# Early products between the steps of the chains: whole groups of eight tiles at every second place in place of half groups at each

## What is computed

```python
for l in range(2):
    z = rmsnorm(x) @ w_in[l]          # all branches and merge gates
    o_a = gated_delta_rule(...)       # branch A: 4 heads, triangular solve in chunks
    o_b = latent_attention(...)       # branch B: 8 heads, prompt causal, samples over 2048 past tokens
    o_c = mlstm_chunked(...)          # branch C: 4 heads
    x += w_out(sum_b sigmoid(gate_b) * (o_b @ w_branch_b))
    x += down(silu(causal_dwconv3(gate) + bias) * up)
```

## Time and profile before

| | |
|---|---|
| median of 3 runs | 1474.86 us (1474.51 to 1476.02) |
| the profiled execution | 1478.7 us, its span 1476.9 us |
| PE busy | 1379.1 us (93%), 7716 matmul records |
| DVE busy | 491.4 us (33%) |
| ACT busy | 273.5 us (19%) |
| POOL busy | 178.4 us (12%) |
| mean granted TensorE clock | 0.973 |

### The profile page before, as it was taken

How to read it: one execution, slowest core, us unless ns; L and a number is a source line. 1 busy time by engine, 2 the same in 40 slices (tenths; PEclk the granted TensorE clock), 3 DMA queues, 4 the chain that set the end, 5 groups by cost and what they waited for, 6 DMA issues and landing times.

```text
span 1476.9 us, 18904 instructions
## 1 busy us (share of the span) xinstructions
PE 1379.1 (93%) x7716; PEld 1140.3 (77%) x7716; DVE 491.4 (33%) x1163; ACT 273.5 (19%) x646; POOL 178.4 (12%) x230
## 2 busy tenths in 40 slices
PE   3999989999999899989989999899999979999894
PEld 3878967777887788878768799677688868888783
DVE  2764255422121333320048434562211223333101
ACT  1331132422100111100014212243220011111000
POOL 1014234120000000000100241442000000000000
PEclk9989999999999999999989899999999999999997
DMA  6422237441343244444444223564224424444320
GB/s 247 143 91 72 86 94 260 162 185 58 121 151 133 100 148 152 142 134 142 140 152 136 69 72 93 194 214 173 99 81 147 137 97 142 152 148 144 133 100 30
DMA packets 58278, 194.82 MB, mean 132 GB/s; under 512 B 7440, under 2 KB 7504, under 8 KB 55120
## 3 DMA queue, kind: packets, MB, share of 16 engines
q1 hardware_dynamic: 49248, 149.97, 30.4%
q0 software_dynamic: 8944, 43.64, 8.5%
HBM read 184.32 MB, written 9.25 MB: 131 GB/s over the span
## 4 chain that ended last, share of the span: by engine, by line
PE 92%; DVE 3%; ACT 2%; issue 1%; DMA 1%; POOL 0%; DVEq 0%; ACTq 0%; POOLq 0%
PE banks L515 70%; PE banks L956 2%; PE banks L634 1%; PE banks L555 1%; PE banks L649 1%; PE banks L962 1%; PE banks L583 1%; PE banks L862 1%; PE banks L1006 1%; PE banks L965 1%; DVE arena L1436 1%; DMA arena<-in_x 1%; PE banks L623 1%; PE banks L950 1%; PE banks L657 1%
## 5 line engine op out<-in xcount | busy, mean ns | idle before, releaser
L515 PE MATMUL banks<-arena 128*128 128x264 f32 x4576 | 1058.4, 391 | 33.8 <-DVE arena L1436 22.8
L515 PEld LDWEIGHTS banks<-arena 128*128 128x128 f32 x4576 | 870.6, 192 | 199.5 <-DVE arena L1436 24.5
L1083 ACT ACTIVATE arena<-banks 128x512 f32<-128x512 f32 (+6 forms) x296 | 119.8, 432 | 524.4 <-PE banks L515 338.9
L1926 DVE TENSOR_SCALAR arena<-arena 128x256 f32<-128x256 f32 x44 | 18.2, 414 | 157.6 <-ACT arena L1083 157.6
L2127 POOL COPY arena<-arena 128x2 f32<-128x2 f32 x44 | 14.0, 317 | 406.3 <-ACT arena L1083 406.3
L1955 DVE SCALAR_TENSOR_TENSOR arena<-banks,arena 128x264 f32<-128x264 f32 x16 | 6.9, 433 | 155.0 <-PE banks L515 155.0
L555 PE MATMUL banks<-arena 128*128 128x264 f32 x64 | 20.6, 490 | 24.3 <-ACT arena L1119 19.3
L2028 POOL TENSOR_TENSOR arena<-arena 128x512 f32<-128x512 f32 x28 | 30.8, 1120 | 84.5 <-PE banks L634 47.3
L555 PEld LDWEIGHTS banks<-arena 128*128 128x128 f32 x64 | 15.5, 249 | 29.0 <-issue 19.7
L1114 ACT ACTIVATE arena<-banks 128x264 f32<-128x264 f32 x32 | 12.6, 392 | 129.4 <-PE banks L515 129.4
L1616 DVE TENSOR_TENSOR arena<-arena,banks 128x512 f32<-128x512 f32 x24 | 16.4, 689 | 55.2 <-PE banks L649 52.6
(11 more groups left out here) (402 smaller groups left out, 1188.5 us busy)
## 6 DMA issues: line engine op xcount, KB each, us to landing
arena<-in_weights SPq DMA_DIRECT2D x230, 512.0 KB, 3.2
arena<-in_weights SPq DMA_DIRECT2D x112, 256.0 KB, 3.1
arena<-in_s POOLq DMA_DIRECT2D x2, 2048.0 KB, 13.0
out_ss_o<-arena POOLq DMA_DIRECT2D x16, 256.0 KB, 3.2
arena<-in_mla_w POOLq DMA_DIRECT2D x4, 1024.0 KB, 8.2
arena<-in_c POOLq DMA_DIRECT2D x4, 512.0 KB, 6.0
out_sc_o<-arena POOLq DMA_DIRECT2D x16, 128.0 KB, 2.7
arena<-in_x POOLq DMA_DIRECT2D x1, 1056.0 KB, 11.2
```

The lines of the kernel that those rows point to most:

```text
L515: mm = nc.tensor.matmul(dst, ring[:, at_:at_ + 128], rhs[:, j, :], start=(start and j == 0), stop=(stop and j == k - 1))
L1083: return A(dst, src, ACT.Copy, scale=scale)
L1926: link(ts(cv, fc[:, j % 3, 0:TP], w[0], par[:, Q_FB + j:Q_FB + j + 1], ALU.mult, ALU.add))
```

## The change

A class `Owed` counts the halves that are due and those that are done. `half(n)` adds n to those due, and then does only as many as make whole groups; a half that is left over is owed until the next place. The same rule stands in `schedule()` and in the blocks of PE, ACT and DVE. Since `wa` and `wc` are single halves, where they come the count shifts by one.

```diff
+class Owed:
+    def __init__(self):
+        self.due = self.done = 0
+
+    def take(self, n):
+        self.due += n
+        at = self.done
+        while at < len(PIECES):
+            end = at + 1 + LAST_PIECE[at:].index(True)
+            if end > self.due:
+                break
+            at = end
+        n, self.done = at - self.done, at
+        return range(n)
...
-                piece, early = [0], [None]
+                piece, early, owed = [0], [None], Owed()
 
                 def half(n):
 
-                    for _ in range(n):
+                    for _ in owed.take(n):
                         k = piece[0]
                         name, i, parts, _ = PIECES[k]
...
-                half(len(PIECES) - piece[0])
+                half(len(PIECES) - owed.due)
                 b = claim("ov", 0, ("cmb", 1))
```

More of the change, by code:

```diff
@@ L89 @@
 assert sorted(STREAM) == list(range(2 * UNITS))
+class Owed:
[11 more added lines that the diff above has]
+        return range(n)
 def schedule():
-    s, piece = [], [0]
+    s, piece, owed = [], [0], Owed()
     def add(name, n=1, reader="A", first=0):
@@ L154, in schedule @@
     add("ss", 1, "A", 1); half(2); add("mxT", 1, "V", 1); half(1); add("mxB", 1, "V", 1); half(3); add("ptx", 1, "A", 1)
-    half(1); add("lsum", 1, "V", 1); add("cx", 1, "A", 1); half(3); add("cmb", 1, "V", 1); half(len(PIECES) - piece[0])
+    half(1); add("lsum", 1, "V", 1); add("cx", 1, "A", 1); half(3); add("cmb", 1, "V", 1); half(len(PIECES) - owed.due)
     add("ov")
@@ L1083, in copy @@
                     return A(dst, src, ACT.Copy, scale=scale)
-                piece = [0]
+                piece, owed = [0], Owed()
                 def half(n):
-                    for _ in range(n):
+                    for _ in owed.take(n):
                         name, i, _, reader = PIECES[piece[0]]
```

## The result

The changed kernel takes 1510.19 us (median of four runs, 1509.28 to 1511.77), the kernel before 1475.44 beside it (four runs, 1474.51 to 1476.3). The ratio is 1.0233, with a 95% interval of 1.022 to 1.0247: slower by 34.7 us. The forecast was 1500.2, with a range of 1490 to 1508; the direction is right, the size too small by 10 us.

A forecast was written before the change was run, and what follows sets the result against it. PE was taken to bound the kernel, its waits paid in full. Lost cover of 11.0 us a layer, +22 for both, plus 3.3 of clock gave 1504.0 for the profiled execution and 1500.2 for the median, range 1490 to 1508.

The forecast's parts named there:

- `l2`, +1.78: From `l2` to the broadcasts: PE's 1.89 us wait grows by the whole moved half, +1.78 us a layer.
- `T` to `TT`, 0.6 each: Levels 1, 3 and 5: `TT`'s second chunk waits for DVE's copy, 0.6 us each, +1.8 a layer.
- `ks` to `vn1`, +1.4: `vn1` is reached at 186.35 but must wait for DVE's four operations, ending at 187.68: +1.4 us a layer.
- `os` to `mn0`, +1.78: PE's 4.05 us wait for DVE ahead of `mn0` grows by the half moved behind `mc1`, +1.78 us a layer.
- `mq`, -0.3: Between `mout` and `mq` two halves stand where one was, so the 0.3 us wait goes: -0.3 a layer.
- `mxT`, +1.4: `mxT` of page 3 has one half fewer ahead and waits for DVE's maximum: +1.4 us a layer.
- the rival by the weight loads: Each of nine uncovered places outside the long waits costs 0.15 us more, 2.8 over both layers: 1503; no chance given.
- the clock: Low clock after the grown waits at `l2` and `mn0`, two in each layer: 0 to 6.6 us in all, +3.3 taken.
- against the runs: Profiled execution lay 3.8 us above the median, so 1504.0 for it was put at 1500.2 for the median.
- only the long waits count: Rival: places at `TT`, `vn0`, `vn1` and the pages are free, 4.8 us a layer: 1484.4, with some clock 1486; 8%.
- More low clock: Rival: every grown wait brings one more low stretch and `l2` two, 22 + 10 = 32 us: 1507; 12%.
- Faster: Rival: clock returns at once or low stretches fall into longer waits, 9.3 us won: 1471.6; 2%.

The follow-up runs named there:

- chain kernel: Kernel before with only the halves in the seven levels and at `vn0`, `ks`, `vn1` made whole groups; traces from `vT` to `o1` take 4.56 and 4.90 us more.
- second trace: Both kernels run again unchanged in a later sitting: the kernel before 1476.5 us (ratio 1.0002), the changed kernel 1511.76 us (ratio 1.024).
- four part kernels: Kernel before with one part each: half behind `l2` moved, half ahead of `mn0` moved, levels to `vn1` whole, or pages whole; together 40.4 us slower.

## Why the prediction fell short

Step by step, with the starts of the steps in layer 0:

1. *`l2`, +1.78*: 1.78 of cover, right, with 0.65 of low clock beside it.
2. *`Y` to `T`, +0.1 for both*: 0.06 and 0.07. Right.
3. *`T` to `TT`, 0.6 each*: 0.63, 0.63, 0.62. Right. In layer 1 the one at level 3 costs 0.34 more, in the chain kernel too: its second chunk waits 0.59 us for 0.23, with the granted clock at 1.00. No run shows why DVE is later there.
4. *`vn0`, +1.0*: 1.05. Right.
5. *`ks` to `vn1`, +1.4*: 1.48. Right; all four operations of DVE count.
6. *`os` to `mn0`, +1.78*: 1.78, right, with 0.22 of clock.
7. *`mq`, -0.3*: -0.15. The half's cover was mis-sized by 0.15.
8. *`mxT`, +1.4*: 1.56 of cover, and, in the first trace, **1.6 of low clock that the term didn't have**. The prediction gave clock to "four places", two in each layer; this is a third in each. In the second trace layer 1 has it and layer 0 doesn't.
9. *Pages 6 and 7, 1.0 each*: 0.95 and 0.94. Right.

Without clock that is 1.78 + 0.13 + 1.88 + 1.05 + 1.48 + 1.78 - 0.15 + 1.56 + 1.89 = 11.4 us a layer for a forecast 11.0; with the 0.34 of layer 1 it is 23.1 for "+22". The moved halves that should "gain none" gain and lose none (the middle: +0.8 us, interval over zero). The start of 0.1 us behind the operand holds, so the rival by the weight loads, 0.15 more at each place, doesn't: `vn0`, `vn1` and the scores of pages 6 and 7 are off their terms by 0.08 at most. The Trainium skill (TensorE: Matmul & The Clock Gate, Architectural detail) says that weight loads can be pulled ahead of running matmuls; losing that lead to a wait costs nothing more here that these terms show.

**The step that failed is "the clock"**: +3.3, with an end at 6.6, counted more low clock only at the four grown waits and put the rest of the program at nothing. The second traces of the two kernels, whose difference (36.1 us, -2.19 to +33.93) is near that of the medians, divide it so: 28.3 us in the touched stages, of which 23.1 is cover and 5.2 clock, and 8.5 behind the two `n2`, all clock; 0.7 less in the rest. That is some 13 us of clock for 3.3. The four grown waits alone have 3.7 of it (0.6 and 0.0 at `l2`, 0.2 and 2.9 at `mn0`), close to the term; `mxT` of layer 1 has 1.5, and the 8.5 behind `n2` are what the term lacked. In the first pair it is 0.9 in the stages and 6.2 behind `n2`: 1.7 at the four waits and 1.6 at each `mxT`, less what before lost at page 0 and the changed kernel didn't. How much of the 8.5 belongs to the change stays open: one execution with 1.78 us of work added has none of it behind the first `n2`, and the changed kernel's first trace has 1.71 there.

**The other failed step is "against the runs"**. It took 3.8 us off the forecast, as if both kernels' medians lay equally far from their profiles. Before's profiled execution is 3.3 over its median, the changed kernel's 0.9 under. The sum for the profiled execution, 1504.0, stands against 1509.28. Of the miss of 10.0 us (1510.19 for 1500.2) the traces have 5.3: 3.8 of clock, 1.1 of cover, 0.4 in the rest. This step has the other 4.7: the 3.8 that it took off, and 0.9.

Of the rivals, *only the long waits count* is refuted by the chain kernel (4.56 and 4.90 us in its stage). *More low clock* (1507, "every grown wait brings one more low stretch and `l2` two") was nearest in size, but that is luck: at the four places the first trace has 0.65 and 0.70 (`l2`), 0.22 and 0.14 (`mn0`), the second 3.7 in all, where it had 10; more of it went where no wait had grown, to `n2`, and to `mxT`. *Faster*, by low stretches that fall into longer waits, did not win, though single pieces moved so: in page 0 of each layer the changed kernel's first trace is 1.66 us shorter than before, which had low clock there (in layer 0 a granted clock of 0.68 from 304.41 to 309.70), and the chain kernel won its 1.52 at `mn0`.

The Trainium skill's rule (TensorE: Matmul & The Clock Gate, Part 1), that the clock falls after idling and returns after sustained work, agrees with the low clock behind the waits of 3.9 and 5.9 us in the changed kernel. But the 2.52 us wait at `n2` was followed by 5.52 us or by 3.84 for the same work, so the rule alone gives no number for this change.

## What to carry to other kernels

Where one engine bounds, filler between dependent steps pays by being at each place, not by its amount: list the places, read from the timelines when the operand lands and when the place is reached, and the sum comes within 5% here (22 for 23.1). Price the clock as a term for the whole program, not for the changed places: with the waits moved, untouched stretches were longer by up to 4.6 us, so a single part's time (8.8 us for 3.6 of cover) says more than its cover, and parts don't add. Against that, repeat the trace, several times for each program, before a difference of some us is explained by a place or by a shift; and put uncovered filler into the waits that are left, which made this kernel 1.4% faster.

## What was not expected of the hardware

Low clock often costs in pieces that are much alike: 1.6 us at `mxT`, 1.7 at the sums `n2`, and behind them none or more, with 1.7 to 4.6 in a stretch. Not all are multiples: behind the second `n2` the four part kernels lose 2.81, 1.97, 2.52 and 1.75 us. The level in a piece is the lower one of 1.2 GHz, as in the earlier trace rows; behind `n2` of the changed kernel:

```profile
493.00:494.00 1.00, 1.00 (x4) 0.77 (x3) 0.00 (x0) 0.18 (x1) 0.00 (x0) 0.50 0.00 0
```

These windows of the changed kernel hold such pieces with some time at full speed around them (columns as above): at `l2`, at `mn0`, behind `mxT`, at `n2`, and behind the waits of 5.7 and 4.2 us that follow in the layer.

```profile
99.00:111.00 12.00, 10.81 (x43) 8.53 (x44) 7.48 (x21) 2.17 (x8) 0.00 (x0) 0.57 0.01 2
212.00:220.00 8.00, 4.62 (x21) 3.89 (x22) 3.93 (x5) 0.98 (x2) 6.18 (x2) 0.57 0.00 0
342.00:346.00 4.00, 4.00 (x21) 3.83 (x20) 1.53 (x3) 2.28 (x6) 0.00 (x0) 0.57 0.01 2
492.00:496.00 4.00, 4.00 (x11) 3.12 (x12) 0.00 (x0) 1.18 (x1) 0.00 (x0) 0.57 0.00 0
502.00:506.00 4.00, 2.87 (x7) 2.25 (x8) 1.08 (x3) 0.00 (x0) 0.00 (x0) 0.58 0.14 35
666.00:670.00 4.00, 4.00 (x12) 3.13 (x11) 0.00 (x0) 0.00 (x0) 0.00 (x0) 0.57 0.37 131
```

A wait of 1.40 us ahead of the short steps `mxT` and `mxB` was followed by such a piece in seven layers of ten, and not in layer 0 of the changed kernel's second trace and of its two traces with products added. The waits of 0.2 to 1.2 us at the levels, `vn0` and `vn1` of the changed kernel were followed by none (granted clock 1.00 from `vT` to `o1` in both layers). And two executions of the kernel before differ by 2.2 us up to the start of PE's last norm sums, with 0.96 of it at `l2` and 1.43 at `mn0` of layer 1, so one trace alone does not give a kernel's clock losses.
